# A two-layer decoder trunk: activation table, norm factors, softmax of the choices and one merge moved

## The reference, cut to what matters

```python
h = rmsnorm(x, norm1_g[l]) * (1 + sc1) + sh1
x = x + g1 * token_mixer(h, ...)   # merged @ w_out,  merged = sig(gate_a)*ya + sig(gate_b)*yb
h = rmsnorm(x, norm2_g[l]) * (1 + sc2) + sh2
x = x + g2 * peer(h, ...)          # top-16 of 16 x 16 candidate pairs per head and token, softmax
                                   # over the 16, then 128 x 128 experts: gelu(h u) * gate, times v
# after the last layer: rmsnorm(x, final_g)
```

## Time and profile before

| what | value |
|---|---|
| time, median of 3 runs | 2181.05 us (2179.7 to 2184.7) |
| time of the profiled execution | 2182.47 us |
| its span | 2180.5 us |
| PE busy | 2105.1 us, 97% of the span |
| DVE busy | 1664.0 us, 76% |
| ACT busy | 1196.6 us, 55% |
| POOL busy | 359.7 us, 16% |
| mean granted PE clock | 0.991 of full speed |

### The profile page before, as it was taken

One profiled execution on the slowest core, in us unless ns is written; L12 is line 12 of the kernel. 1 busy time (PEld: TensorE's weight loads), 2 busy tenths in 40 slices (PEclk: granted clock), 3 DMA queues, 4 the chain that ended last, 5 costly groups with the idle time before them and its releaser, 6 DMA issues.

```text
span 2180.5 us, 41571 instructions
## 1 busy us (share of the span) xinstructions
PE 2105.1 (97%) x14556; PEld 1950.7 (89%) x14556; DVE 1664.0 (76%) x3066; ACT 1196.6 (55%) x2161; POOL 359.7 (16%) x260
## 2 busy tenths in 40 slices
PE   3999899999999999999989999999999999999998
PEld 2899899999999988888879998999999998888886
DVE  7786869998788788888665865899977886666665
ACT  2468455546666544555556664554476664555554
POOL 0000000000999400000000000000059990000000
PEclk7999999999999999999999999999999999999999
DMA  7764645555444488888654444555544345555653
GB/s 310 259 219 144 206 162 176 183 183 174 134 132 132 164 289 289 289 290 287 230 181 157 157 141 168 165 183 180 181 151 136 127 135 173 192 192 192 192 192 116
DMA packets 114184, 412.47 MB, mean 189 GB/s; under 512 B 13264, under 2 KB 13904, under 8 KB 113424
## 3 DMA queue, kind: packets, MB, share of 16 engines
q1 hardware_dynamic: 114064, 410.86, 56.5%
HBM read 406.48 MB, written 1.57 MB: 187 GB/s over the span
## 4 chain that ended last, share of the span: by engine, by line
PE 90%; DVE 4%; ACT 3%; POOL 1%; DMA 1%; issue 1%; SPq 0%; DVEq 0%; ACTq 0%
PE ps L1435 32%; PE ps L1132 15%; PE ps L1136 15%; PE ps L1133 15%; PE ps L1414 5%; PE ps L1201 2%; ACT w_hi L430 1%; PE ps L1184 1%; POOL hot L416 1%; DVE w_lo L689 1%; PE ps L1356 1%; PE ps L1389 1%; PE ps L1290 1%; DVE big L764 1%; DVE big L743 1%
## 5 line engine op out<-in xcount | busy, mean ns | idle before, releaser
L689 DVE TENSOR_TENSOR w_lo<-raw,w_hi 128x1024 fp32r<-128x1024 f32 x664 | 811.9, 1223 | 287.6 <-ACT w_hi L430 283.2
L430 ACT CAST w_hi<-raw 128x1024 fp32r<-128x1024 f32 x664 | 695.1, 1047 | 560.1 <-PE ps L1136 491.1
L1132 PE MATMUL ps<-h_hi,w_hi 128*128 128x256 f32 x2912 | 723.6, 286 | 1.9 <-ACT big L435 1.7
L1133 PE MATMUL ps<-h_lo,w_hi 128*128 128x256 f32 x2912 | 713.6, 283 | 0.0
L416 POOL TENSOR_SCALAR hot<-con,rt 128x128 f32<-128x128 f32 x256 | 359.5, 1415 | 1438.3 <-DVE neg L1076 1410.7
L1132 PEld LDWEIGHTS ps<-h_hi,w_hi 128*128 128x128 f32 x2912 | 557.6, 191 | 6.0 <-issue 2.6
L1133 PEld LDWEIGHTS ps<-h_lo,w_hi 128*128 128x128 f32 x2912 | 558.2, 192 | 0.1
L1136 PE MATMUL ps<-h_hi,w_lo 128*128 128x256 f32 x2912 | 409.1, 283 | 4.3 <-DVE w_lo L689 4.3
L1136 PEld LDWEIGHTS ps<-h_hi,w_lo 128*128 128x128 f32 x2912 | 375.5, 192 | 5.0 <-DVE w_lo L689 4.9
L621 ACT CAST p_hi<-big 128x256 fp32r (+1 forms) x256 | 103.8, 406 | 343.0 <-PE ps L1435 343.0
L1435 PE MATMUL ps<-w_hi,p_hi 128*128 128x512 f32 x1024 | 274.9, 389 | 0.2
(11 more groups left out here) (185 smaller groups left out, 1687.5 us busy)
## 6 DMA issues: line engine op xcount, KB each, us to landing
raw<-in_u SPq DMA_DIRECT2D x256, 512.0 KB, 3.5
raw<-in_v SPq DMA_DIRECT2D x256, 512.0 KB, 4.4
raw<-in_win SPq DMA_DIRECT2D x104, 512.0 KB, 3.9
hot<-in_ada SPq DMA_DIRECT2D x80, 512.0 KB, 3.9
raw<-in_wq SPq DMA_DIRECT2D x32, 512.0 KB, 3.5
big<-in_ada SPq DMA_DIRECT2D x16, 512.0 KB, 14.6
raw<-in_wout SPq DMA_DIRECT2D x16, 512.0 KB, 4.1
big<-in_decay SPq DMA_DIRECT2D x2, 1536.0 KB, 12.0
```

Of the source, the lines that this page charges most:

```text
L430: nc.scalar.copy(w_hi[:, j % 2, :], raw[:, j, :]).then_inc(hi_ready, 1)
L689: tt(w_lo[:, j % 2, :], raw[:, j, :], w_hi[:, j % 2, :].bitcast(F32), ALU.subtract).then_inc(lo_ready, 1)
L1132: mm(o, w, h_hi[:, k, :], start=(k == 0), stop=False)
L1133: mm(o, w, h_lo[:, k, :], start=False, stop=False)
```

## The change: what it does

1. `root_table()`, the one-element reciprocal square root, is taken out of `squares` except at q = 0. On ACT it now stands in the `w_out` stage behind the rounding of block 56 (k == 2), four roundings earlier, and at the end of a layer before the last four blocks of `v`.
2. `gains` moves out of `norm`: behind the `w_out` loop, before the updates of x; at the end of a layer before the updates of x; the last layer's factor likewise.
3. `merge(3)` moves behind the low half of block 53.
4. The softmax of the choices is split: shift at m = 71, sum and normalisation at m = 72, behind the low half of block 73.
5. `MOD_AT` has 2 and 45 in place of 51 and 57. As each load and each reduction goes by its place in this list, block k = 2 is now reduced at m = 2 instead of 3, k = 3 at 3 instead of 5, k = 4 at 5 instead of 7, and so on up to k = 17; the last ones are at 54, 55 and 56.

```diff
-MOD_AT = (0, 1, 3, 5, 7, 9, 12, 14, 16, 18, 19, 21, 23, 25, 27, 42, 43, 47, 49, 51, 54, 55, 56, 57)
+MOD_AT = (0, 1, 2, 3, 5, 7, 9, 12, 14, 16, 18, 19, 21, 23, 25, 27, 42, 43, 45, 47, 49, 54, 55, 56)
...
+            def root_table():
+                nc.scalar.activation(small[:, 0, 3, 0:1], eps, ACT.Abs_reciprocal_sqrt)
             def squares(q):
-                nc.scalar.activation(small[:, 0, 3, 0:1], eps, ACT.Abs_reciprocal_sqrt)
+                if q == 0:
+                    root_table()
...
                 for k in range(N_WOUT - 1):
                     round_hi(l * N_BLOCKS + B_WOUT + k + 2, (k + 2) % RING)
+                    if k == 2:
+                        root_table()
...
                 st.loop(N_V // RING - 1, 0, outputs)
+                root_table()
                 outputs(N_V // RING - 1, end=True)
...
                 if q:
-                    gains(l, gain, sc, 0, KC)
                     rstd_chain(q)
...
                 merged_lo(1)
-                merge(3)
                 for k in range(N_WOUT - 1):
                     low(l * N_BLOCKS + B_WOUT + k + 1, (k + 1) % RING)
+                    if k == 0:
+                        merge(3)
                     if k < 2:
                         merged_lo(k + 2)
                     mod_at(B_WOUT + k)
+                gains(l, V_N2 + KC * l, SC2, 0, KC)
...
                         nc.vector.tensor_copy(gt, shift_w).then_inc(shifted, 1)
+                    if m == N_U1 + 1:
                         dve.wait_ge(exped, l + 1)
                         us.link(nc.vector.tensor_reduce(sums, gt, AX_X, ALU.add))
...
+                if l + 1 < DEPTH:
+                    gains(l + 1, V_N1 + KC * (l + 1), SC1, 0, KC)
+                else:
+                    st.link(ts(alpha[:], vec[:, V_FIN:V_FIN + KC], RSTD_FACTOR, None, ALU.mult))
                 for k in range(KC):
                     dve.wait_ge(y_turned, KC * l + k + 1)
...
-            st.link(ts(alpha[:], vec[:, V_FIN:V_FIN + KC], RSTD_FACTOR, None, ALU.mult))
```

## The result

| | before | changed |
|---|---|---|
| median, 12 runs each | 2181.51 us | 2186.51 us |
| lowest to highest | 2179.23 to 2184.7 | 2183.56 to 2190.88 |
| profiled execution, span | 2182.47, 2180.5 | 2186.45, 2184.5 |

The ratio is 1.0026, 95% interval 1.0018 to 1.0033. I had forecast 2178.8 (2174.5 to 2182.5). It moved the other way, and lies outside the range.

A forecast was written before the change was run, and what follows sets the result against it. PE, with work in 97% of the span, was taken as the bound, so only its own waits could give time back. Terms -2.4 - 1.9 + 0.6 - 0.2 + 1.6 = -2.3 us gave 2178.8 us (range 2174.5 to 2182.5).

The forecast's parts named there:

- Root's table: At the end of each layer, PE's 1.20 us wait for the first square goes: -2.4 us in all.
- Rival 1: At the very end the clock stays at 2.4 GHz: 1.7 us more gained, 2177.0 us; chance 0.2.
- Norms behind w_out: PE's waits for the first square in both layers and for block 59's low half in layer 0 go: -1.9 us.
- Norm factors: Two instructions of 0.16 and 0.17 us now run while DVE waits for PE: nothing either way.
- Merge: Blocks 53 and 54: the w_lo wait becomes one on w_hi, about 1.8 us; +0.1 in layer 0, +0.5 in layer 1.
- Softmax: PE's 1.68 us wait for block 73's low half goes, but is given back at the gates: -0.1 us a layer.
- Mods: Near 65 us, block 5's low half stands behind late mod block 3: a new PE wait, +1.6 us.
- Rival 3: First stage: the mod ring chokes it, mod block 3 and one weight block late; +1.4 us, 2182.5 us; chance 0.1.

The follow-up runs named there:

- e8: The kernel before with two extra DVE tensor_reduce (one SBUF operand) behind the copies that start POOL; timed once, 2182.84 us.
- e1: The kernel before with only the softmax of the choices split over two steps; 2186.21 us against 2181.44, ratio 1.0024.
- e2: The kernel before with only the last merge moved behind the low half of block 53; 2184.21 us against 2181.44, ratio 1.0013.
- e3: The kernel before with the new MOD_AT alone; 2182.14 us against 2181.44, ratio 1.0003.
- e5: The kernel before with the softmax split and all gates one block later; 2177.46 us against 2181.56, ratio 0.9983.
- e6: The kernel before with the merge moved and, on ACT, block 54's rounding ahead of the last merged part; 2178.42 us against 2181.56, ratio 0.9987.
- e7: The kernel before with two extra DVE tensor_tensor (two SBUF operands) behind the copies that start POOL; timed once, 2185.54 us.
- e11: The kernel before with 45 in place of 57 in MOD_AT and no early 2; timed once, 2181.65 us.
- e4: The kernel before with only root's table loaded ahead and the norm factors made ahead; 2176.55 us against 2181.44, ratio 0.9976.
- e9: The changed kernel with all gates one block later; 2179.2 us against 2181.22 for the kernel before, ratio 0.9988.
- e12: The changed kernel again, with no edit, for a second profile; timed once, 2189.1 us.

## Why the prediction was wrong, step by step

**Root's table: right.** -1.2 a layer end was forecast; -1.3 and, less the clock, -1.2 came. The square sum starts at 1106.12 in the changed kernel, on the old count 1102.2, where the prediction has it. Rival 1 (the clock holds at the end, -1.7) came true. But it came true in every profile except those of before and e8, also in those that keep the wait of 1.20 us there (e1, e2, e3, e5, e6, e7, e11). So what happens there hangs on more than PE's idle time before it.

**Norms behind w_out: right**, -1.9 forecast, -2.3 measured. Norm factors: nothing seen, as forecast; they were not timed apart from the table.

**Merge: the mechanism right, a cost left out.** The prediction says "a wait of 1.5 us is turned into another, on w_hi, of about 1.8". It is 1.74. What I left out is that the new wait brings down the clock and the old one did not. The term "+0.5" and "+0.1" came out as +2.1 and +1.7.

**Softmax: the step that failed.** "Its eight one-hot rows take 10.48 us and end at 552.8", and from it "PE gives the 1.6 us back at gates 0 and 1". This takes the length of POOL's work from a profile in which DVE stood idle for the first 1.0 us of it, and carries it to a schedule in which this gap is gone. The gap was made by the very wait that the split removes. POOL's start was forecast to 0.13 us; its speed was not a property of POOL. And the step reads the end of the eighth row alone, while the first gate waits for the fourth. The eight rows came out only 0.5 us longer, the first four 2.3 (7.1 us, not 4.8), and so PE waits 2.67 us at the first gate. The term "-0.1 a layer" came out as +2.8: -1.2 at the softmax, +2.3 or so from POOL, and 1.7 from the clock. At the softmax itself PE gained 1.2 and not 1.6, since it then waits 0.5 us for ACT's gelu. e1 shows the term alone, e5 shows it gone with the gates one block later, and e7 and e8, with the rows of all profiles, show what holds POOL up. I wrote that PE gives the 1.6 us back; I should have asked what they do to DVE, which also gets ahead.

**Mods: right in kind**, +1.6 forecast, +1.8 to +2.2 by the wait alone, because the low half of block 6 is late too (69.84 on PE, 3.07 us behind block 5's instead of 2.88). The wait itself was 1.62, 1.3 to 2.2 over the four profiles with this list. Rival 3 (the ring chokes the stage) did not come: nothing behind block 6 lags.

**The clock.** I counted it only at the very end. With four falls more and one fewer, 3 x 1.7 = 5.1 us of the profiled difference of 4.0 are clock, and -1.1 is left for everything else. Of my -2.3, the split was -0.2; by the table, less the clock, it came to 2 x (2.3 - 1.2) = +2.2, which makes the sum +0.1. The other terms of the table came out 0.6 better than forecast, and 0.6 lie in the small steps that it leaves out.

**Open.** Why the clock falls behind a given wait in one run and not in the next is not settled; the length of the wait alone doesn't decide it, as e2's 2.14 us and e4's 3.1 us without a fall show. Whether the last fall is in most runs of the kernel before or only in its profiled one, no run tells, and with it how much of e4's, e5's and e6's gains it is.

## What to carry to other kernels

When a wait is removed, go through every engine that gets ahead by it, and ask what ran undisturbed in the gap that the wait had made. A duration read in a trace holds for what ran beside it; on POOL look at what DVE does in the same microseconds, and at the row that the first consumer waits for, not at the sum. And where PE's wait is only moved, its price is the wait and perhaps 1.7 us of slower clock behind it: leave slack at the receiving end (one block later for the gates, one rounding earlier for block 54) before pulling anything forward.

## What the runs showed of the hardware

- A POOL tensor_scalar of 128x128 takes 0.80 us with DVE idle, beside a tensor_reduce with one SBUF operand, or beside a tensor_tensor of 128x1024 with one input in PSUM. It takes 2.89 us when two tensor_tensor of 128x1024 with two SBUF operands start beside it, and 0.79 when it starts 0.1 us or more ahead of them.
- A fall of the granted clock to 0.50 in the middle of the kernel cost 1.6 to 1.8 us of PE's time where PE had work throughout.
- The clock fell behind waits of 1.74 us and held behind others of 2.14 and 3.1 us. The same kernel had it fall at four places outside the norms in one profile and at five in the other.
- The load of mod block 3 is issued up to 0.8 us earlier or later against PE's matmuls in four profiles with the same list (the changed kernel, e3, e9, e12), and PE's wait near 65 is 1.3 to 2.2 us.
